# The attention of a second block: meta tokens' scores taken apart, a step more of scores in flight, projections moved

## The reference, cut to what matters

```python
sc = jnp.einsum('bqkgd,blkd->bkgql', qg, ka) * scale        # kind A: 8 heads of 64, 2 key heads
p = jax.nn.softmax(sc, axis=-1)
o = jnp.einsum('bkgql,blkd->bqkgd', p, va)

sc = jnp.einsum('bqhjd,blhjd->bhjql', q, kb) * scale        # kind B: 4 heads, two maps (j) each
p = jax.nn.softmax(sc, axis=-1)
w = p[:, :, 0] - lam * p[:, :, 1]
o = rms_norm(jnp.einsum('bhql,blhe->bqhe', w, vb), subln_g) * (1.0 - lam_init)

x = x + jnp.einsum('ble,ed->bld', concatenate([out_a, out_b]), w_out)
```

## Time and profile before

| What | us |
|---|---|
| median of 3 runs | 2457.68 (2456.47 to 2461.82) |
| profiled execution, its own time | 2463.03 |
| its span | 2461.2 |
| PE busy in the span | 2318.0 (94%) |
| POOL busy | 1474.4 (60%) |
| DVE busy | 1074.8 (44%) |
| ACT busy | 610.4 (25%) |

### The profile page before, as it was taken

The page is one execution under the profiler, slowest core; times in us unless marked ns, Lnnn a source line. Parts: engine busy times, 40 slices in busy tenths (PEclk is TensorE's granted clock), DMA queues, the critical chain, the costliest instruction groups (busy, mean ns, idle before and its releaser), DMA issues.

```text
span 2461.2 us, 30592 instructions
## 1 busy us (share of the span) xinstructions
PE 2318.0 (94%) x10971; PEld 1853.4 (75%) x10971; DVE 1074.8 (44%) x1623; ACT 610.4 (25%) x1058; POOL 1474.4 (60%) x1452
## 2 busy tenths in 40 slices
PE   5989999999999998898999999999998879999998
PEld 4666788788888886666888888888876446788887
DVE  7794772543321148847725332211382552433200
ACT  3323423321110023234233211110242551211100
POOL 5563645687677745535456866766492216776673
PEclk9999999999999998999999999999999989999999
DMA  3321223422322322212234222222331002222222
GB/s 124 118 69 52 85 72 101 154 94 96 100 94 96 101 95 92 69 52 69 82 99 156 94 102 94 94 91 97 116 112 44 1 0 69 86 95 101 94 94 77
DMA packets 68516, 217.35 MB, mean 88 GB/s; under 512 B 8256, under 2 KB 8384, under 8 KB 68288
## 3 DMA queue, kind: packets, MB, share of 16 engines
q1 hardware_dynamic: 52528, 187.72, 23.2%
q10 hardware_dynamic: 15888, 28.21, 3.2%
HBM read 195.93 MB, written 10.49 MB: 84 GB/s over the span
## 4 chain that ended last, share of the span: by engine, by line
PE 82%; DVE 12%; ACT 4%; issue 1%; DMA 1%; ACTq 0%; POOL 0%; SPq 0%; DVEq 0%; POOLq 0%
PE ps L1530 71%; PE ps L1797 2%; PE ps L1955 2%; ACT pe L937 2%; DVE score L1323 1%; DVE small L1319 1%; DVE b_sb L1380 1%; PE ps L1714 1%; DVE h_lo L1028 1%; PE ps L1747 1%; PE ps L1732 1%; DVE small L1208 1%; PE ps L1758 1%; DVE htb L1023 1%; PE ps L2012 1%
## 5 line engine op out<-in xcount | busy, mean ns | idle before, releaser
L502 POOL TENSOR_TENSOR w_lo<-w_raw,w_hi 128x512 fp32r<-128x512 f32 x700 | 955.0, 1364 | 58.4
L499 POOL TENSOR_SCALAR w_hi<-w_raw 128x512 fp32r<-128x512 f32 x700 | 497.9, 711 | 759.1 <-DMA w_raw<-wst 726.3
L1530 PE MATMUL ps<-h_hi,w_lo 128*128 128x512 f32 (+1 forms) x2048 | 807.4, 394 | 29.6 <-DVE h_lo L1028 17.3
L1530 PE MATMUL ps<-h_lo,w_hi 128*128 128x512 f32 (+1 forms) x2048 | 787.7, 385 | 0.0
L1530 PE MATMUL ps<-h_hi,w_hi 128*128 128x512 f32 (+1 forms) x2048 | 787.7, 385 | 0.0
L1530 PEld LDWEIGHTS ps<-h_hi,w_lo 128*128 128x128 f32 x2048 | 389.5, 190 | 130.8 <-issue 23.2
L1530 PEld LDWEIGHTS ps<-h_lo,w_hi 128*128 128x128 f32 x2048 | 390.5, 191 | 78.5 <-issue 6.2
L1530 PEld LDWEIGHTS ps<-h_hi,w_hi 128*128 128x128 f32 x2048 | 389.7, 190 | 76.5
L1530 PE MATMUL ps<-a_hi,w_lo 128*128 128x512 f32 (+1 forms) x572 | 214.3, 375 | 0.0
L1530 PE MATMUL ps<-a_lo,w_hi 128*128 128x512 f32 (+1 forms) x572 | 213.9, 374 | 0.0
L1530 PE MATMUL ps<-a_hi,w_hi 128*128 128x512 f32 (+1 forms) x572 | 213.8, 374 | 0.0
(11 more groups left out here) (277 smaller groups left out, 2661.2 us busy)
## 6 DMA issues: line engine op xcount, KB each, us to landing
w_raw<-wst SPq DMA_DIRECT2D x350, 512.0 KB, 3.5
rot<-raw ACTq DMA_DIRECT2D x70, 128.0 KB, 2.1
gates<-gt ACTq DMA_DIRECT2D x32, 256.0 KB, 4.1
stage<-gates ACTq DMA_DIRECT2D x32, 256.0 KB, 3.5
x_sb<-xin SPq DMA_DIRECT2D x4, 512.0 KB, 8.0
out<-x_sb SPq DMA_DIRECT2D x1, 2048.0 KB, 7.1
kc<-cst ACTq DMA_DIRECT2D x1, 1056.0 KB, 4.9
kc<-cst ACTq DMA_DIRECT2D x1, 481.0 KB, 5.0
```

The costliest lines, as they stand in the source:

```text
L499: eng.tensor_scalar(w_hi[s][:, part], w_raw[s][:, part], 1.0, 1.0, ALU.mult, ALU.mult)\
L502: eng.tensor_tensor(w_lo[s][:, part], w_raw[s][:, part], w_hi[s][:, part].bitcast(F32), ALU.subtract)\
L1530: m = eng.matmul(o, w, x, start=first and i == 0, stop=final and i == 2)
```

## The change

The 16 meta keys leave the steps. PE takes the scores of all steps with them at once, behind step 0's scores, into two banks of PSUM; DVE copies them to `m_sb` and takes their maxima in two operations for all steps (`nmeta`). In each step DVE joins the two maxima, subtracts the joint one from the step's meta scores, ACT takes a small exponential of them, and DVE adds up their sums for the reciprocal. The scores of a step now fill two whole banks, and there are two such pairs, used in turn: PE waits for the exponentials of step t - 2. LAG becomes 3. In DVE's loop `inverse_sums(t - 1)` moves behind `maxima(t)`. POOL splits half a chunk of the output weights behind each odd step of B, wo2 to wo5 in all. The projections over k = 0 to 3 stand ahead of the last step's transposes, k = 4 and 5 behind them, k = 6 behind the last values, then the last norm's sum, then k = 7. In B the copy of the result to `osb2` on ACT goes; the square and the scaling read PSUM. Cut to its core:

```diff
-LAG = 2
+LAG = 3
-        def score_tile(u, i):
-            at = 0 if i == 0 else 1024 - META + 512 if u < PAIRS_A else 1024
-            return ps[:, at:at + TM]
+        def score_tile(t, i):
+            return bank(2 * (t % 2) + i)
...
 POOL, softmax_weights:
                         eng.tensor_scalar(x, x, small[:, 33 + c:34 + c], small[:, 52:53], ALU.mult, ALU.mult)\
                            .then_inc(p1_ready, 1)
+                        if b % 2:
+                            h = (t - TB * PAIRS_A) // 2
+                            c = index[(L2, "wo2")] + h // 2
+                            if h % 2 == 0:
+                                eng.wait_ge(w_dma[c % WSLOTS], 16 * (c // WSLOTS + 1))
+                                eng.sem_inc(w_seen, 1)
+                            split_half(c, c % WSLOTS, h % 2)
...
 ACT, exps:
+                eng.wait_ge(nm2_ready, t + 1)
                 for i in range(2):
-                    s, col = 2 * t + i, 8 * (u % 2) + 2 * b + i
-                    eng.wait_ge(nm2_ready, s + 1)
-                    eng.activation(pe[u % 2][:, 2 * b + i, :], score_tile(u, i), ACT.Exp,
+                    col, at = 8 * (u % 2) + 2 * b + i, META * i if u < PAIRS_A else 0
+                    eng.activation(pe[u % 2][:, 2 * b + i, at:at + T], score_tile(t, i), ACT.Exp,
                                    bias=small[:, col:col + 1], accum_out=small[:, 16 + col:17 + col])\
                        .then_inc(e2_ready, 1)
+                eng.wait_ge(md2_ready, t + 1)
+                eng.activation(meta_cols(t), meta_cols(t), ACT.Exp).then_inc(em2_ready, 1)
...
-                eng.activation(osb2[:, :], bank(7), ACT.Copy).then_inc(y2_taken, 1)
-                eng.wait_ge(y2_taken, h + 1)
-                eng.activation(osq2[:, :], osb2[:, :], ACT.Square).then_inc(osq2_ready, 1)
+                eng.activation(osq2[:, :], bank(7), ACT.Square).then_inc(osq2_ready, 1)
...
 DVE:
+            def meta_scores():
+                eng.wait_ge(mk2_ready, 1)
+                for i in range(2):
+                    eng.tensor_copy(m_sb[:, i, :], bank(6 + i)).then_inc(mk2_taken, 1)
+                eng.wait_ge(mk2_taken, 2)
+                for i in range(2):
+                    k = step(eng.tensor_reduce(nmeta[:, i:64:2], m_sb[:, i, :].rearrange("p (t m) -> p t m", m=META),
+                                               AX.X, ALU.max, negate=True))
+                after(k)
+
             def maxima(t):
                 u, b = divmod(t, TB)
+                col, at = 8 * (u % 2) + 2 * b, 80 + 2 * (t % 2)
                 for i in range(2):
-                    col = 8 * (u % 2) + 2 * b + i
                     eng.wait_ge(s2_ready, 2 * t + i + 1)
-                    eng.tensor_reduce(small[:, col:col + 1], score_tile(u, i), AX.X, ALU.max, negate=True)\
-                       .then_inc(nm2_ready, 1)
+                    k = step(eng.tensor_reduce(small[:, at + i:at + i + 1], score_tile(t, i), AX.X, ALU.max, negate=True))
+                if t == 0:
+                    meta_scores()
+                after(k)
+                eng.tensor_tensor(small[:, col:col + 2], small[:, at:at + 2], nmeta[:, 2 * t:2 * t + 2], ALU.min)\
+                   .then_inc(nm2_ready, 1)
+                eng.wait_ge(nm2_ready, t + 1)
...
+                less = small[:, col:col + 2].rearrange("p (i o) -> p i o", o=1).to_broadcast([P, 2, META])
+                eng.tensor_tensor(meta_cols(t), m_sb[:, :, META * t:META * (t + 1)], less, ALU.add).then_inc(md2_ready, 1)
 
             def inverse_sums(t):
-                eng.wait_ge(e2_ready, 2 * t + 2)
+                c, at = 8 * (u % 2) + 2 * b, 84 + 2 * (t % 2)
+                eng.wait_ge(em2_ready, t + 1)
+                after(step(eng.tensor_reduce(small[:, at:at + 2], meta_cols(t), AX.X, ALU.add)))
+                after(step(eng.tensor_tensor(small[:, 16 + c:18 + c], small[:, 16 + c:18 + c], small[:, at:at + 2], ALU.add)))
                 eng.reciprocal(small[:, 32 + c:34 + c], small[:, 16 + c:18 + c]).then_inc(inv2_ready, 1)
...
             for t in range(STEPS + LAG + TB):
-                if 0 < t <= STEPS:
-                    inverse_sums(t - 1)
                 if t < STEPS:
                     maxima(t)
                 if 0 < t <= STEPS:
+                    inverse_sums(t - 1)
                     difference(t - 1)
...
 PE:
             def scores_2(t):
-                eng.wait_ge(e2_ready, 2 * t) if t else None
...
+                if t < 2:
+                    for i in range(2):
+                        taken(eng, (L2, f"vb{2 * t + i}"))
+                else:
+                    eng.wait_ge(e2_ready, 2 * t - 2)
+                for i in range(2):
+                    rows = slice(64 * i, 64 * i + 64)
+                    eng.matmul(score_tile(t, i), qab[rows, u, b * P:(b + 1) * P], kab[rows, keys_of(u), 0:T],
+                               start=True, stop=True).then_inc(s2_ready, 1)
+            def meta_scores():
+                taken(eng, (L2, "vbm"))
+                for t in range(STEPS):
+                    u, b = divmod(t, TB)
                     for i in range(2):
                         rows = slice(64 * i, 64 * i + 64)
+                        m = eng.matmul(bank(6 + i, META * t, META), qab[rows, u, b * P:(b + 1) * P],
+                                       kab[rows, keys_of(u), T:TM], start=True, stop=True)
+                m.then_inc(mk2_ready, 1)
...
+            def first_outputs(ks):
+                if ks[0] == 0:
+                    eng.wait_ge(e2_ready, 2 * STEPS)
+                cs = [chunk((L2, f"wo{i}")) for i in range(4)]
+                for k in ks:
+                    eng.wait_ge(ysp_lo, 8 * L2 + k + 1)
+                    for i in range(4):
+                        m = product(bank(i), *weights(cs[i], k), h_hi[:, k, :], h_lo[:, k, :], k == 0, k == KT - 1)
...
             for t in range(STEPS + LAG + 1):
                 if t < STEPS:
                     scores_2(t)
+                if t == 0:
+                    meta_scores()
                 u, b = divmod(t - LAG, TB)
+                if t == STEPS + 2:
+                    first_outputs(range(4))
                 if b == 0 and u:
                     values(u - 1)
...
+                if t == STEPS + 2:
+                    first_outputs(range(4, 6))
+            first_outputs(range(6, 7))
+            o_square_2(HH - 1)
+            first_outputs(range(7, 8))
             for i in range(4, KT):
                 gemm((L2, f"wo{i}"))
```

More of the change, by code:

```diff
@@ L410, in program @@
         nm2_ready = sem("nm2_ready")
+        mk2_ready = sem("mk2_ready")
+        mk2_taken = sem("mk2_taken")
+        md2_ready = sem("md2_ready")
+        em2_ready = sem("em2_ready")
         e2_ready = sem("e2_ready")
@@ L493, in _, with split_half @@
             rounds = len(chunks) // WSLOTS
+            def split_half(c, s, i):
+                part = slice(512 * i, 512 * (i + 1))
+                eng.tensor_scalar(w_hi[s][:, part], w_raw[s][:, part], 1.0, 1.0, ALU.mult, ALU.mult)\
+                   .then_inc(w_top, 1)
+                eng.wait_ge(w_top, c * 2 + (i + 1))
+                eng.tensor_tensor(w_lo[s][:, part], w_raw[s][:, part], w_hi[s][:, part].bitcast(F32), ALU.subtract)\
+                   .then_inc(w_ready, 1)
             def split(c, s, landed):
@@ L497, in split @@
                 eng.sem_inc(w_seen, 1)
[L498 to L503 removed]
+                for i in range(2):
+                    split_half(c, s, i)
             def softmax_weights():
@@ L541, in _ @@
             softmax_weights()
-            done = between
+            done = between + 4
             splits(done, len(chunks))
@@ L1943, in scores_2, with keys_of @@
                 u, b = divmod(t, TB)
-                if t == 0:
-                    for i in range(TB):
-                        taken(eng, (L2, f"vb{i}"))
-                eng.wait_ge(e2_ready, 2 * t) if t else None
-                keys = 0 if u < PAIRS_A else 1 + u - PAIRS_A
-                for part in (slice(0, T), slice(T, TM)):
+                if t < 2:
[3 more added lines that the diff above has]
+                    eng.wait_ge(e2_ready, 2 * t - 2)
+                for i in range(2):
+                    rows = slice(64 * i, 64 * i + 64)
+                    eng.matmul(score_tile(t, i), qab[rows, u, b * P:(b + 1) * P], kab[rows, keys_of(u), 0:T],
+                               start=True, stop=True).then_inc(s2_ready, 1)
+            def keys_of(u):
+                return 0 if u < PAIRS_A else 1 + u - PAIRS_A
+            def meta_scores():
+                taken(eng, (L2, "vbm"))
+                for t in range(STEPS):
+                    u, b = divmod(t, TB)
                     for i in range(2):
                         rows = slice(64 * i, 64 * i + 64)
-                        metas_first = i == 1 and u < PAIRS_A
-                        at = part.start if not metas_first else 0 if part.start else META
```

(19 more changed lines are left out.)

28 lines of the change are left out of this document (14 added, 14 removed).

## The result

The changed kernel takes 2476.53 us (median of 4 runs, 2473.43 to 2481.60), the kernel before 2458.25 in the same comparison (4 runs, 2456.47 to 2461.82): a ratio of 1.0075, with a 95% interval of 1.0053 to 1.0096. It is slower, by 18 us where 5.4 were forecast, and 2476.5 lies just outside the range, which ended at 2476. The profiled execution, the longest of the four, took 2481.6 around a span of 2479.8; that of the kernel before, above all four of its runs, took 2463.03 around 2461.2.

A forecast was written before the change was run, and what follows sets the result against it. A queue of dependent work, no full engine, was taken to bound the second block's attention. Terms +5.4 - 3.2 + 1.7 + 1.8 + 3.1 + 2.0 - 5.4 = +5.4 us gave 2463 us, range 2450 to 2476.

The forecast's parts named there:

- part 5: TensorE's clock falls in the sparse steps t = 16 to 31: 1.1 us added to each of two units.
- part 3: Value steps, t = 0 to 15: unit of four steps 16.46 us instead of 17.53, three units saving 3.2.
- Part 1: Start-up: 64 small meta-key matmuls (9 us) and DVE's copies and reductions delay the first exponential; 5.4 us lost.
- Part 2: DVE's chain in plain steps, t = 0 to 15: two steps in flight, step falls from 3.56 to 2.73 us.
- R3: Rival: DVE's small operations cost 0.4 us rather than 0.2, plain steps stay near 3.6; 2472 us, chance 0.10.
- Part 4: Steps t = 16 to 31 lengthen because DVE's difference waits 0.92 us for POOL's scaling; unit 21.5 us.
- R2: Rival: in steps t = 16 to 31 values, transposes and norm run at half clock; +9 us, 2472, chance 0.20.
- Part 6: The end, last unit's values until the first four projections are done: 41.5 us instead of 46.9, gain 5.4.
- Part 7: Edits priced at nothing: POOL's splitting of wo2 to wo5 and ACT's removed copy of the result.
- R1: Rival, faster: DVE's wait for POOL doesn't decide the pace in steps t = 16 to 31; 2453 us, chance 0.20.
- R4: Rival: start cheaper and last norm short, no pause of clock; 2459 us, no change, chance 0.12.

The follow-up runs named there:

- kernel 3: Changed kernel with the 64 small meta-key matmuls issued earlier, ahead of the last chunk of the value projection: 2474.9 us, ratio 1.0059 to the kernel before.
- kernel 7: Changed kernel with the small meta-key matmuls in two parts, eight behind step 0's scores, 56 behind step 1's: 2474.53 us, ratio 1.0057 to the kernel before.
- kernel 1: Changed kernel with DVE's difference taken one turn later, t - 2 instead of t - 1: 2464.99 us, ratio 1.0022 to the kernel before.
- kernel 2: Changed kernel with the score matmuls of steps t = 16 to 31 issued three times, except right behind values: 2472.42 us, ratio 1.0051 to the kernel before.
- Kernel 4: Changed kernel with the end projections reordered, so two rounds of products follow the last norm's sum: 2472.03 us, ratio 1.0039 to the kernel before.
- kernel 8: Changed kernel with later difference, reordered end projections, next step's scores ahead of values, and small meta matmuls in two parts: 2452.12 us, ratio 0.9963 to the kernel before.
- kernel 9: As kernel 8, with the score matmuls of steps t = 16 to 31 issued three times: 2451.42 us, ratio 0.9965 to the kernel before.

## Why the prediction was wrong

The sign, and the mechanism named first, were right: DVE waits 0.92 us for POOL in every step of B. The size was a third of what came (5.4 of 16.0 in the stretch). The step that failed is the price of TensorE's clock, too small in part 5 and, with it, at the start and in the end; a smaller share is a wait that part 3 left out. By the prediction's own parts:

- *Part 1, start-up, forecast +5.4, measured +8.4.* The 64 matmuls lasted 10.45 us against the 9 taken, inside the bounds of 6.8 and 13.7, but not for either bound's reason: at full clock each record added 0.056 us (67 from 1886.24 to 1890), at half clock 0.10 (65 in 6.60 us). At 0.056 us each the 128 records would take 7.2 us, an estimate from these rows, so at full clock the 9 was not too low; the excess is the clock's. The half clock also lasted beyond them, through the scores of steps 2 and 3 (3.79 us for two groups at 1901.28), so the second step came 3.6 us behind the first instead of 2.5. Another 0.5 us was lost before V0 by the wait of part 3. Kernels 3 and 7 show that the price follows the matmuls wherever they stand.
- *Part 2, DVE's step 2.73.* Measured 2.70 where nothing holds it (maxima at 1925.17 and 1927.87, DVE's timeline). Right, and R3, dearer small operations, is refuted: they lasted 0.16 to 0.19 us. (R3's own product, 5 x 0.2 x 25, is 25 us, not 20.)
- *Part 3, A units 16.46, measured 16.98.* Missed: the transposes of all steps go into the same banks, so those of one step wait until ACT has copied those of the step before (`t2_taken`, L975), and they stand in front of the next scores in PE's queue. ACT makes that copy behind its exponentials. The part had PE's scores wait for exponentials alone, and left this wait out.

```profile
1928.21 0.59 ACT L975 ACTIVATE pt2a<-ps 128x512 f32<-128x512 f32 x1
...
1928.95 1.06 PE L2022 MATMUL ps<-kc,pe 128*128 128x128 f32 x8 [1.73 <-POOL pe L530]
...
1929.94 1.13 PE L1992 MATMUL ps<-kab,qab 64*128 64x512 f32 x4
...
1930.16 1.39 POOL L530 TENSOR_SCALAR pe<-pe,small 128x528 f32<-128x528 f32 x2 [1.31 <-DVE small L1257]
...
1930.85 0.59 ACT L975 ACTIVATE pt2a<-ps 128x512 f32<-128x512 f32 x1
...
1931.55 0.85 PEld L2022 LDWEIGHTS ps<-kc,pe 128*128 128x128 f32 x8 [1.31 <-POOL pe L530]
```

The brackets name POOL, and that is misleading. The transposes at 1928.95 are those of step 6, and they need POOL's scaling of step 6, which had ended at 1921.46, 7 us earlier. POOL's scaling at 1930.16 is that of step 8 and ended at 1931.55, when PE's loads for step 7 already began; ACT's copies ended 0.11 us ahead of PE's loads both times (1928.80 to 1928.92, 1931.44 to 1931.55). The scores behind the transposes put the maxima of step 10 3.23 us behind those of step 9 instead of 2.73: the 0.5 us of each unit.

- *Part 4, B steps.* Forecast 5.72, 4.42 and 4.75 between the maxima of V4's unit and 0.15 to V5; measured 5.69, 4.41, 4.74 and 0.18. Each step was right within 0.03 us. On the contention, the odd difference lost 0.34 us beside POOL's first split operation (1.11 against 0.77), not the whole 0.62.

```profile
2005.19 0.62 POOL L509 TENSOR_SCALAR w_hi<-w_raw 128x512 fp32r<-128x512 f32 x1
```

  The difference had started at 2005.26 and ended 0.56 us behind POOL's operation. In kernel 1 the two-column operation ended 0.02 us behind POOL's subtraction, and POOL's scaling at 1983.50 ended 0.66 us behind DVE's difference. Each is 0.12 to 0.21 us less than the bare length (0.77, 0.16 and 0.78). The Trainium skill, page "SBUF — State Buffer", section "SBUF: two separate sides", has the operation that starts second blocked until the other's instruction is over. All three rows agree with it if the first 0.1 to 0.2 us of the blocked operation run all the same, an estimate from these lengths. What doesn't agree is the prediction's use of it, a loss of the other's full length: the two had started 0.07 us apart.
- *Part 5, the clock: the step that failed.* It allowed 1.1 us a unit and only from V4 on. From V4 to the next maxima 9.47 us passed instead of 7.53 (6.43 and the 1.1), all of it in the values and what stands with them, 7.72 us at half clock where 5.8 were taken. V3 to V4, given no clock at all, had 5.35 us values and a clock of 0.83. Kernel 2 shows the cause by putting the clock back. This was rival R2 (chance 0.20, values 7.3, 2472 us). The argument held against it was that full clock had come back within the values in the old trace. But the old windows already had 0.81 to 0.88 in B and 0.75 from V6 on, and the 2.3 us of PE work in a step of 3.56, which the part set beside the new steps, is a step of A: an old step of B had 1.19 of scores and 0.59 of transposes. The new steps hold about as much (1.06 and 0.59), over a longer time.
- *Part 6, the end, forecast 5.4 gained, measured 4.2* (43.1 us from V6 against 47.3, both to the start of the 96th projection matmul). To the end of these matmuls the sum of 41.5 measures 43.3. From V6 to the first product 9.67 us passed at a clock of 0.73, where 8.0 were taken. The exposed norm was as said (4.73 us from the sum's start to the next product, forecast 4.6). The twelve products behind it took 4.41 us at a clock of 0.61, 1.7 more than at full speed, where half of 2.5 was taken. The rest came out 0.4 us shorter. The 46.9 of the old kernel was read 0.6 us short: its 96th matmul starts at 2066.76. Kernel 4 removes the pause and the slow products behind it, 5.5 us, by order alone.
- *Part 7.* Nothing in the traces contradicts it: no load or split was late.

R1 (the wait doesn't decide) is refuted by kernel 1, R4 by part 1. The errors in the forecast of the stretch, in order: 3.0 at the start, 1.7 in A and the two steps before V3, 4.7 in B, 1.2 in the end, 10.6 us together. The clock has a part in all but the 1.7; of the 3.0 at the start 1.4 fell at the small matmuls, 1.1 at the scores of step 2, both by the clock, and 0.5 at part 3's wait. For V3's values, for those of V4 to V6 and behind the last norm the prediction took TensorE faster than it ran, each time behind work that it had itself found sparse.

## What to carry to other kernels

When a change makes the steps of a queue longer while TensorE's work in them stays the same, price the large matmuls behind them by the slowest such row of the old trace (here 6.26 us for the last values; the new ones took 5.35 to 6.74), in the forecast and not in a rival. Check whether matmuls stand between an engine's wait and its next input; if they do, issue the small producers first. A wait that one row of the old trace shows at its bare price, 0.92 us here, held in all sixteen places. A call moved in one engine's list has to be followed into every kind of step: here the same move gained about 2 us a unit in A and lost 4.9 us over three units in B. And a recurrence needs a term for every buffer that is used again: one bank per map, freed by ACT's copy, cost 0.5 us a unit, and the name in the row's brackets pointed elsewhere. Ask which step's work the waiting instruction needs before you believe it.

## What the runs showed that was not expected

- TensorE lost its clock while its rows show it busy without a pause: 6.60 of 6.60 us of 16-column matmuls at a granted clock of 0.50, level 1.2 GHz, right behind 4.7 us at 0.96. With the same matmuls earlier (kernel 3) it happened again, and the products behind them ran at half speed for another 5.3 us (1888.24 to 1893.52). Only the clock column tells; the busy column reads full.
- A two-column DVE operation took 0.76 us instead of 0.16 while POOL's subtraction of two inputs ran, and POOL's scaling 1.22 us instead of 0.78 while DVE's difference ran beside it (kernel 1). In that pairing the difference kept its 0.75: POOL paid.
- 48 more matmuls of 512 columns (kernel 2) made the stretch 6.1 us shorter, because three units' values and scores ran at or near full clock (1.00, 0.93 and 1.00); with the waits removed (kernels 8 and 9), when the values of V4 and V5 took 3.70 us anyway, the same matmuls brought nothing.
